# Seven half products in place of eight for 18 weight pairs of the first layer's feed-forward input, and a folded sequence transform

## The reference

```python
def ffn_sublayer(x, shift, scale, gate, g_pre, g_post, w_ffn_in, w_ffn_out):
    h = modulate(rmsnorm(x, g_pre), shift, scale)
    a, u = jnp.split(h @ w_ffn_in, 2, axis=-1)
    y = (jax.nn.silu(a) * u) @ w_ffn_out
    return x + gate * rmsnorm(y, g_post)

def fourier_mix(u):            # real part of the 2-D DFT over positions and channels, per channel group
    uf = u.astype(jnp.float32).reshape(b, l, FOURIER_GROUPS, w // FOURIER_GROUPS)
    return jnp.fft.fft2(uf, axes=(1, 3), norm="ortho").real
```

## Time and profile before

| | |
|---|---|
| three timed runs | median 1761.64 us (1760.34 to 1761.86) |
| profiled execution | 1760.17 us |
| its span | 1758.4 us |
| granted TensorE clock, mean | 0.976 |
| TensorE busy with matmuls | 1653.8 us (94%) |
| VectorE, ScalarE, GpSimd busy | 666.6 us, 516.1 us, 572.2 us |

### The profile page before, as it was taken

How to read it: one execution, slowest core, us unless ns; L and a number is a source line. 1 busy time by engine, 2 the same in 40 slices (tenths; PEclk the granted TensorE clock), 3 DMA queues, 4 the chain that set the end, 5 groups by cost and what they waited for, 6 DMA issues and landing times.

```text
span 1758.4 us, 22457 instructions
## 1 busy us (share of the span) xinstructions
PE 1653.8 (94%) x9084; PEld 1330.8 (76%) x9084; DVE 666.6 (38%) x847; ACT 516.1 (29%) x752; POOL 572.2 (33%) x259
## 2 busy tenths in 40 slices
PE   5899999999899999999999988999988899999995
PEld 1677877876688888888888746888765688888884
DVE  2510226768721211211111795126747422122136
ACT  3524113523522111221122245342422422222220
POOL 1412222134423222232222443233213444444432
PEclk9899999999899999999999999999999999999998
DMA  9334332135321121111211373122153233333331
GB/s 373 140 125 155 120 135 93 37 132 195 121 81 60 61 71 61 60 60 63 69 60 60 108 260 137 49 84 73 61 204 108 61 97 94 95 97 94 95 105 62
DMA packets 46331, 185.18 MB, mean 105 GB/s; under 512 B 4854, under 2 KB 7798, under 8 KB 39608
## 3 DMA queue, kind: packets, MB, share of 16 engines
q1 hardware_dynamic: 42444, 172.63, 29.7%
q10 hardware_dynamic: 3820, 11.60, 1.7%
HBM read 175.83 MB, written 8.39 MB: 105 GB/s over the span
## 4 chain that ended last, share of the span: by engine, by line
PE 61%; issue 19%; DVE 8%; POOL 5%; ACT 2%; DMA 2%; SPq 1%; POOLq 0%; DVEq 0%; ACTq 0%
PE A L636 55%; POOL w_lo L591 5%; DVE x L1327 2%; DVE y L1334 1%; DVE y L1326 1%; PE A L808 1%; PE A L802 1%; DMA raw<-modw 1%; DVE h_lo L1339 1%; PE N L873 1%; DVE sqb L1301 1%; PE G L777 1%; PE A L816 1%; ACT h_hi L1076 1%; SPq L555 1%
## 5 line engine op out<-in xcount | busy, mean ns | idle before, releaser
L591 POOL TENSOR_TENSOR w_lo<-raw,w_hi 128x1024 fp32r<-128x1024 f32 (+1 forms) x219 | 524.6, 2397 | 1074.4 <-ACT w_hi L897 1074.3
L636 PE MATMUL A<-h_hi,w_hi 128*128 128x512 f32 (+1 forms) x1808 | 571.0, 363 | 30.0 <-DVE h_lo L1339 21.3
L636 PE MATMUL A<-h_lo,w_hi 128*128 128x512 f32 (+1 forms) x1808 | 559.4, 357 | 0.0
L636 PE MATMUL A<-h_hi,w_lo 128*128 128x512 f32 (+1 forms) x1808 | 558.4, 356 | 0.0
L897 ACT ACTIVATE w_hi<-raw 128x1024 fp32r<-128x1024 f32 (+1 forms) x219 | 228.1, 1042 | 818.4 <-PE A L636 781.9
L636 PEld LDWEIGHTS A<-h_hi,w_hi 128*128 128x128 f32 x1808 | 306.7, 190 | 107.5 <-issue 27.9
L636 PEld LDWEIGHTS A<-h_lo,w_hi 128*128 128x128 f32 x1808 | 309.1, 191 | 49.3 <-issue 0.2
L636 PEld LDWEIGHTS A<-h_hi,w_lo 128*128 128x128 f32 x1808 | 307.3, 191 | 51.4
L1311 DVE TENSOR_TENSOR sqb<-sqb,A 128x768 f32<-128x768 f32 (+1 forms) x44 | 36.1, 821 | 427.2 <-PE A L636 426.9
L636 PE MATMUL A<-g_hi,w_hi 128*128 128x512 f32 (+1 forms) x528 | 168.5, 359 | 1.0 <-DVE y L1298 0.4
L636 PE MATMUL A<-g_hi,w_lo 128*128 128x512 f32 (+1 forms) x528 | 167.4, 356 | 0.0
(11 more groups left out here) (131 smaller groups left out, 1157.4 us busy)
## 6 DMA issues: line engine op xcount, KB each, us to landing
raw<-stream SPq DMA_DIRECT2D x219, 512.0 KB, 3.5
mraw<-modw SPq DMA_DIRECT2D x42, 1024.0 KB, 5.1
raw<-modw SPq DMA_DIRECT2D x6, 1024.0 KB, 14.8
x<-x_keep ACTq DMA_DIRECT2D x4, 1536.0 KB, 8.9
x_keep<-x SPq DMA_DIRECT2D x4, 768.0 KB, 21.4
x<-xT SPq DMA_DIRECT2D x1, 2048.0 KB, 8.5
x_keep<-x ACTq DMA_DIRECT2D x2, 1024.0 KB, 9.3
out_dram<-x ACTq DMA_DIRECT2D x4, 512.0 KB, 2.8
```

The costliest lines, as they stand in the source:

```text
L591: pool.tensor_tensor(w_lo[:, n % RING, 0:WIDTH[n]], raw[:, n % RAW, 0:WIDTH[n]], w_hi[:, n % RING, 0:WIDTH[n]].bitcast(F32), ALU.subtract) ...
L636: m = pe.matmul(dst[:, t0:t1], a, b[:, k, t0:t1], start=(first and p == 0), stop=(last and p == 2))
```

## The change

**Feed-forward input of the first layer.** The first four pairs stay as they are. For each of the other 18 the K axis (1024) and the 768 tokens are halved, and the two weight tiles `a` and `u` form the third halving: a 2 x 2 times 2 x 2 product. It is done by Strassen's method in Winograd's form: seven products of a weight quarter (512 x 128) with an activation quarter (512 x 384), each in three passes over four K tiles, 84 matmuls of 384 columns. Four weight sums (`w_sum`) are made for each pair and four activation sums T1 to T4 once. The seven results go round through eight PSUM banks and are joined by additions. Both weight tiles of a pair lie in the two `raw` buffers, from a new array `pairs`.

```diff
+FAST = 4
+LOW_P, LOW_S = (0, 1, 2, 5, 6), (3, 4)
+READ_ACT, READ_DVE = (0, 3), (1, 2, 4, 5, 6)
@@ SyncE, in its loop over the chunks
+                    if n == n_out(b):
+                        sp.wait_ge(lo_done, n)
+                        for pair in fast_pairs(b):
+                            q = pair - FAST
+                            if q:
+                                sp.wait_ge(f_lo, 5 * q)
+                                sp.wait_ge(sums_ready, 4 * q)
+                            for j in range(2):
+                                sp.dma_start(raw[:, j, :], pairs[q, :, j, :]).then_inc(pair_in, 16)
@@ GpSimd
+                        for pos in LOW_P:
...
+                            pool.wait_ge(f_hi, 7 * q + pos + 1)
+                            if pos == 2:
+                                pool.wait_ge(sums_ready, 4 * q + 4)
+                            pool.tensor_tensor(lo, src, f_weight(w_hi, q, pos).bitcast(F32), ALU.subtract).then_inc(f_lo, 1)
@@ TensorE
+                    moving = [h_block(0, 0), h_block(1, 0), t_block(2), h_block(0, 1), t_block(3), h_block(1, 1), t_block(4)]
+                    def product(q, pos):
...
+                        for k in range(4):
+                            cols = slice(k * P, (k + 1) * P)
+                            for a, b, p in ((wh, hi, 0), (wh, lo, 1), (wl, hi, 2)):
+                                m = pe.matmul(dst, a[:, cols], b[:, k, :], start=(k == 0 and p == 0),
+                                              stop=(k == 3 and p == 2))
+                        m.then_inc(f_used, 1)
...
+                        if i == 0:
+                            for u in ("A0", "A1") if e[2] else ("A0", "A1", "N0", "N1", "G0", "G1"):
+                                pe.wait_ge(free[u], PLAN.acc[e][u])
@@ TensorE, ffn_out
+                    if L == 0:
+                        pe.wait_ge(f_got, 2 * (sum(BLOCKS[:e[2] + 1]) - FAST))
+                        pe.wait_ge(f_sum, 5 * (sum(BLOCKS[:e[2] + 1]) - FAST))
@@ ScalarE, one pair
+                act.wait_ge(f_used, at + 1)
+                act.activation(part, bank(q, 0), ACT.Copy).then_inc(f_got, 1)
+                if not last:
+                    fast_hi(q + 1, 0)          # waits for pair_in of pair q + 1
+                act.wait_ge(f_used, at + 2)
...
+                act.wait_ge(f_used, at + 4)
+                act.wait_ge(g_ready, q + FAST + 1)
+                act.activation(up[:, hi_half], bank(q, 3), ACT.Copy).then_inc(f_got, 1)
+                    for pos in (2, 3, 4):
+                        fast_hi(q + 1, pos)
+                act.wait_ge(f_sum, summed(q, 5))
+                act.activation(sil[:, 0:TOK], sil[:, 0:TOK], ACT.Silu).then_inc(f_silu, 1)
+                act.wait_ge(f_used, at + 6)
+                    fast_hi(q + 1, 5)
+                act.wait_ge(f_used, at + 7)
+                    fast_hi(q + 1, 6)
+                act.wait_ge(f_gated, q + 1)
+                act.activation(g_hi[:, gp:gp + 1, :], sqb[:, 0:1, :], ACT.Copy).then_inc(ghi_ready, 1)
@@ VectorE, one pair
+                dve.tensor_tensor(sil[:, lo_half], part, bank(q, 1), ALU.add).then_inc(f_sum, 1)
+                dve.tensor_tensor(part, part, bank(q, 2), ALU.add).then_inc(f_sum, 1)
+                    dve.wait_ge(f_used, at + 4)
+                    early_sums(q + 1)          # 2 of 512, wait for pair_in of pair q + 1
+                step(dve.tensor_tensor(sil[:, hi_half], part, up[:, hi_half], ALU.add), 1)
+                dve.tensor_tensor(part, part, bank(q, 4), ALU.add).then_inc(f_sum, 1)
+                    late_sum(q + 1, 4)
+                step(dve.tensor_tensor(up[:, hi_half], part, up[:, hi_half], ALU.add), 2)
+                dve.tensor_tensor(sil[:, hi_half], sil[:, hi_half], bank(q, 5), ALU.add).then_inc(f_sum, 1)
+                    late_sum(q + 1, 5)
+                    sum_low(q + 1, 3)
+                    sum_low(q + 1, 4)
+                dve.tensor_tensor(up[:, lo_half], part, bank(q, 6), ALU.add).then_inc(f_sum, 1)
+                dve.tensor_tensor(sil[:, 0:TOK], sil[:, 0:TOK], up, ALU.mult).then_inc(f_gated, 1)
+                dve.tensor_tensor(g_lo[:, gp:gp + 1, :], sqb[:, 0:1, :], g_hi[:, gp:gp + 1, :].bitcast(F32),
+                                  ALU.subtract).then_inc(g_ready, 1)
```

**Room for the sums.** T2 and T3 lie where `x` is, so `x` is written to DRAM before the feed-forward block and read back at its last `ffn_out`. VectorE waits for that write before its first activation sum, and that stands ahead of its part of the first pairs:

```diff
+                elif kind == "spill":                                     (ScalarE, behind tail(0, 0))
+                    for s in range(0, KT, 4):
+                        act.dma_start(x_keep[:, s:s + 4, :], x[:, s:s + 4, :]).then_inc(x_kept, 16)
+                elif kind == "ffn_in" and L == 0:                         (VectorE)
+                    dve.wait_ge(x_kept, 96)
...
+                    t_sums(1)          # 4 x 384 elements each
+                    t_sums(3)
+                    t_sums(2)
+                    for q in range(FAST):
...
```

**Folded sequence transform.** Cosine and sine sums of a real sequence are even and odd in the output position. The `dft` chunks now hold only 258 of 512 (130 of 256) columns, the two sums go into PSUM columns of their own, and VectorE joins them:

```diff
-                    w = CTX if ctx_part else SEQ
+                    w = HALF_CTX if ctx_part else HALF_SEQ
@@ ORDER, among the attention tiles
             order.append(("score", L, tt))
+            if a == 0:
+                order.append(("halves", L))
...
             order.append(("o", L, tt))
+            if a == 0:
+                order.append(("fold", L))
```

More of the change, by code:

```diff
@@ L46, with fast_pairs, normal_pairs @@
 PB, PG, PCW, PCB, PGN, PCOLS = 0, 48, 80, 86, 88, 92
+FAST = 4
+HALF = TOK // 2
+LOW_P, LOW_S = (0, 1, 2, 5, 6), (3, 4)
+READ_ACT, READ_DVE = (0, 3), (1, 2, 4, 5, 6)
+def fast_pairs(b):
+    first = sum(BLOCKS[:b])
+    return range(max(first, FAST), first + BLOCKS[b])
+def normal_pairs(L, b):
+    first = sum(BLOCKS[:b])
+    return range(first, min(first + BLOCKS[b], FAST) if L == 0 else first + BLOCKS[b])
 def tiles_of(L):
@@ L215, in build_order @@
         tail(L, 0)
+        if L == 0:
+            order.append(("spill", 0))
         first = 0
         for b, nb in enumerate(BLOCKS):
-            order.append(("ffn_in", L, b, first))
+            if normal_pairs(L, b):
+                order.append(("ffn_in", L, b, first))
+            if L == 0:
+                order.append(("fast", L, b))
             order.append(("ffn_out", L, b))
@@ L240, in chunks_of @@
         out = []
[L241 removed]
+        for p in normal_pairs(L, e[2]):
             out += [("fin", L, p), ("fin", L, HID + p)]
@@ L374, in piece_before, with bass_hybrid_block @@
 def piece_before(p):
+    if PIECES[p][1:3] == (1, 1) and PIECES[p][3] < 2:
+        return PLAN.n0[("ffn_out", 0, 2)] + RAW + RING
     return PLAN.n0[PIECES[p - 2]] + RAW + RING - 1
-def bass_hybrid_block(nc: bass.Bass, stream, modw, xT, pos_row, pos_col, cols, wdec, masks, mats, wide, x_keep, out):
+def bass_hybrid_block(nc: bass.Bass, stream, pairs, modw, xT, pos_row, pos_col, cols, wdec, masks, mats, wide, x_keep, out):
     with ExitStack() as ctx:
@@ new lines, in y_block, with h_block, t_block, n_out @@
+        def y_block(k2, t2):
+            return y[:, 4 * k2:4 * k2 + 4, HALF * t2:HALF * t2 + HALF]
+        def h_block(k2, t2):
+            return [t[:, 4 * k2:4 * k2 + 4, HALF * t2:HALF * t2 + HALF] for t in (h_hi, h_lo)]
+        def t_block(j):
+            return [t[j] for t in (T_hi, T_lo)]
+        def n_out(b):
+            return PLAN.n0[("ffn_out", 0, b)]
+        def ring_half(q, pos):
+            b = next(b for b in range(len(BLOCKS)) if q + FAST in fast_pairs(b))
+            h = (2 * (n_out(b) % RING) + pos) % (2 * RING)
+            return h // 2, slice(h % 2 * 512, h % 2 * 512 + 512)
@@ L913, in _, with fast_hi, first_hi @@
             act.wait_ge(eps_set, 1)
+            def fast_hi(q, pos):
+                src = {0: A_RAW[1, 1], 1: A_RAW[1, 2], 6: A_RAW[2, 2]}
+                if pos in src:
+                    act.wait_ge(pair_in, 32 * (q + 1))
+                else:
+                    act.wait_ge(sums_ready, 4 * q + {3: 2, 2: 2, 4: 3, 5: 4}[pos])
+                src = src.get(pos, ring_f(q, pos))
+                act.activation(f_weight(w_hi, q, pos), src, ACT.Copy).then_inc(f_hi, 1)
+            def first_hi(b, step):
+                act.wait_ge(chunk_used, n_out(b) - 3 + step)
+                for pos in ((0, 1), (2, 3), (4, 5), (6,))[step]:
+                    fast_hi(fast_pairs(b)[0] - FAST, pos)
@@ L978, in _ @@
                 elif kind == "dft":
-                    end = e[2] == (3 if L else 4)
-                    if not end:
+                    if chunk_kind(n0 + RING) == "dft":
                         high(n0 + RING)
@@ L1435 @@
         "stream": stream_layout(a),
+        "pairs": pair_layout(a),
         "modw": mod_layout(a),
```

365 lines of the change are left out of this document (325 added, 40 removed).

## The result

| | before | after |
|---|---|---|
| timed runs | 1761.75 us median of 4 (1760.34 to 1762.37) | 1777.88 us median of 4 (1771.77 to 1781.81) |
| ratio, 95% interval | | 1.0087 (1.0070 to 1.0104) |
| profiled execution, granted clock | 1760.17 us, 0.976 | 1771.77 us, 0.969 |
| TensorE busy | 1653.8 us | 1623.5 us |

TensorE has 30 us less to do, and the program is 11.6 us longer in the profiled execution, 16 in the median. The chain of waits, by engine, answers to the earlier trace rows: the share of "issue" fell from 19% to 5%, and VectorE (8% before), DMA (2%) and ScalarE (2%) have larger shares, as TensorE itself has (61%).

What follows compares the result with a forecast made beforehand. It took TensorE's own instruction stream to bound the kernel; 1760.2 - 40.7 + 9.6 + 6.2 + 8 + 2 - 7 = 1738.3, and with 1.5 for the median 1739.8 us, range 1720 to 1766.

Steps and rivals of the forecast that it cites:

- term 2: Feeding the 18 pairs: the loop through the `raw` buffers takes 16.3 us, six late pairs lose 9.6 us in all.
- Term 1: The 18 pairs on TensorE: 84 matmuls of 384 columns at 0.175 each, 14.7 us per pair, 40.7 us won.
- rival D: TensorE's clock falls in the fast pairs' gaps of 1.6 us, for a quarter of that time: 1756 us, chance 0.04.
- term 3: Seams at starts and ends of the three pair blocks: TensorE waits for PSUM buffers and last additions, 6.2 us lost.
- Term 4: Writing x to DRAM before the activation sums: TensorE stands 5.9 us before chunk 3, then a slower clock, 8 us lost.
- Term 5: Norm in two steps: four tiles get a second ScalarE instruction, about half hidden in idle time, 2 us lost.
- Term 6: Folded transform in both layers: 11.4 us leave TensorE, 2.2 charged per layer among the attention tiles, 7 us won.
- A: The loop through `raw` never binds, as collisions are rarer or DMAs land sooner: 1730 us, chance 0.24.
- B: VectorE and GpSimd collide at full length, the loop through `raw` takes 19.3 us: 1771 us, chance 0.16.
- C: The fold brings nothing and the gap at the first block is 13 us: 1752 us, chance 0.14.

Runs made afterwards that it cites:

- E1: Third weight-half buffer, in a free part of `mraw`, added to the changed kernel: 1739.36 us, ratio to before 0.9883.
- E11: Changed kernel with two low parts per pair left out on VectorE and filled by two ScalarE copies: 1778.88 us.
- E10: Changed kernel, still with one pair of raw buffers, given finer waits at the six seams: 1762.6 us, ratio to before 1.0006.
- E5: Kernel before with the norm in two steps, x written to DRAM, waited for and read back, no activation sums: 1768.76 us.
- E7: E1's kernel with the activation sums and their wait for x moved behind VectorE's work for pair 0: 1738.28 us.
- E4: Kernel before with only the first layer's second norm done in two steps through `y`: 1768.4 us, ratio 1.0034.
- E8: E7's kernel with the norm in one step again and `y` completed afterwards: 1728.09 us.
- E3: Kernel before with the folded sequence transform alone: 1757.44 us, ratio 0.9979.

## Why the prediction was wrong, step by step

I forecast 1740 us and faster at 0.79. It came out at 1777.88, outside my range of 1720 to 1766, and slower. The step that failed is term 2, and within it the account of when the loop binds.

**Term 1, 18 pairs at 0.175: right.** With the third buffer a pair takes 14.72 us, so its 84 matmuls start 0.175 apart. The 18 pairs bring 39.7 us (305.3 at 16.96, 265.6 in E1's three blocks).

**Term 2, +9.6: measured 31.** The three blocks of pairs, from the first product to the end of the last, take 64.5, 133.3 and 98.8 us, the seam waits of 3.0, 3.0 and 1.3 taken off. In E1's kernel, where no pair waits, the same stretches take 59.1, 118.0 and 88.5, so the loop costs 31 us. Both factors were off. The period is 17.6 where I had 16.3: the fourth sum comes 7.0 after the landing (I said 6.1), the three low parts take 5.3 (4.95), the DMA 5.2 (5.1 + 0.1). Of the first part the collisions are what I had too small: L1452 and L1515 take 2.15 us more than their 0.69 and 0.55, where I had charged 1.0. (The 3.6 us of the chain is right for four instructions of 384; the text counts three.) And the stock in hand was 2.9 us, not 4.6. VectorE makes the early sums of the next pair behind its wait for product 3, so in a block's first pair they begin 2.8 us after the landing. In the second block, whose first product starts at 680.4, the landing is at 686.22 and the sums come here (timelines of VectorE and GpSimd):

```profile
689.06 0.96 DVE L1450 TENSOR_TENSOR w_sum<-raw 128x512 f32<-128x512 f32 x1 [1.53 <-PE G L1035]
...
694.64 3.32 POOL L783 TENSOR_TENSOR w_lo<-w_sum,w_hi 128x512 fp32r<-128x512 f32 x2 [5.17 <-DVE w_sum L1461]
```

The third weight is ready at about 696.4, 16.0 after the first product; I had 14.3. A stock of 2.9 and an excess of 2.9 per pair cover one pair, not three. So the loop binds from the fourth pair of a block (in the first block the third already waits 1.0): ten waits in place of six. The loop, 17.6, lay inside my bounds of 14.0 to 19.3; I had it as "the middle" and let the stock hide what a longer one does.

**Clock falls, 0.04 for rival D: there, but not shown to cost anything.** Windows of 5 to 6 us behind the last pairs' waits of the three blocks:

```profile
597.00:602.00 5.00, 4.89 (x19) 4.92 (x20) 3.85 (x5) 1.22 (x2) 3.62 (x2) 0.66 0.08 12
...
800.00:806.00 6.00, 4.64 (x18) 4.67 (x19) 4.85 (x6) 2.02 (x4) 4.86 (x3) 0.72 0.07 8
971.00:977.00 6.00, 5.90 (x25) 5.93 (x26) 4.52 (x6) 1.23 (x2) 3.61 (x2) 0.72 0.21 59
```

At these clocks the matmuls take about 1.7 us longer in each window. But the end of a block does not hang on them. In E11's profile the granted clock stays at 1.00 behind these three waits, and the blocks' pairs take 289.2 us in place of 296.5; TensorE then waits 13.4 us in place of 7.3 for VectorE's last additions. In the second block the last addition comes at 815.51 there and at 815.68 in the changed kernel. It hangs on the landing of the stream's first chunk (term 3). So what the falls take from term 2 they seem to give back in term 3, and the sum of the two, 31 + 12, is the firmer number. The rule that I weighed for D (the Trainium skill, "TensorE: Matmul & The Clock Gate", A second HAM failure mode) is so far borne out: with gaps of 2.3 us between groups of matmuls the clock falls now and then. In E1's kernel, which goes round the same eight banks without them, it stayed at 1.00 for all three blocks. So the gaps matter and the cycling alone does not. It is not a quarter of the time, as I had priced it.

**Term 3, seams +6.2: measured 12.4**, and 9.0 to 15.3 come back when the waits go (E10). The starts were right (1.2 each). The ends were not: 8.9 us where I had 2.6. The timeline of the first block's last pair:

```profile
604.32 1.06 ACT L1105 ACTIVATE w_hi<-raw 128x1024 fp32r<-128x1024 f32 x1 [3.59 <-issue]
605.29 0.47 ACT L1161 ACTIVATE sqb<-A 128x384 f32<-128x384 f32 x1
605.46 5.05 POOL L743 TENSOR_TENSOR w_lo<-raw,w_hi 128x1024 fp32r<-128x1024 f32 x2 [4.84 <-ACT w_hi L1105]
...
605.79 2.50 DVE L1515 TENSOR_TENSOR sqb<-mrow,sqb 128x384 f32<-128x384 f32 x1 [3.00 <-ACT sqb L1161]
...
608.91 2.02 DVE L1521 TENSOR_TENSOR sqb<-mrow,sqb 128x384 f32<-128x384 f32 x1
```

ScalarE's copy of product 3 (L1161) stands behind `w_hi` of the stream's first chunk, whose DMA is issued only after the pair's last low part. Two additions behind that copy then meet GpSimd's low parts of the stream, 2.50 and 2.02 us, and TensorE stands for 3.05 us until the last addition is done.

**Term 4, spill +8: measured a gap of 2.7**, and 0.4 for write and wait alone (E5). x landed 11.5 after the issue (I said 12), but I held the chunk before it for punctual: TensorE was ready for chunk 3 at 497.6 and not at 492.8, about 5 us late behind the norm in two steps, and that hid half of the stall. With the slower matmuls behind it the stall costs 3.7 us by the stage's length (E7).

**Term 5, norm in two steps +2: measured 6.5** (E4); 10.2 came back in E8, with E7's scatter in it. I took half as hidden in ScalarE's idle time. But TensorE waits tile by tile there, and the clock falls behind it.

**Term 6, fold -7: measured -4.5** (E3), the right sign. Matmuls of 130 columns cost 0.112 each, where I had scaled to 0.068, so 24 of them cost 1.1 us more than I had (rows of the changed kernel below; the earlier trace rows for the stage). The rest is in the attention tiles. In E3's profile the transforms are 5.4 and 5.2 us shorter, but from their start to `wout` only 1.9 and 2.9 are left, so the tiles lose 3.6 and 2.3 where I had charged 2.2 each:

```profile
301.58 0.28 PE L941 MATMUL A<-w_hi,h_lo 128*128 128x130 f32 x1
301.69 0.28 PE L941 MATMUL A<-w_hi,h_hi 128*128 128x130 f32 x1
```

**The sum again**, for the profiled execution: 1760.2 - 39.7 + 31 + 12 (12.4 less the 0.4 of before) + 2.7 + 6.5 - 4.5 = 1768.2 against 1771.8. The missing 3.6 us aren't assigned; 1.7 of them lie between `wout` and the first fast pair. The end of the tail and the head, which answer to the earlier trace rows, stood at a clock of 0.75:

```profile
462.00:489.00 27.00, 21.48 (x92) 17.18 (x91) 16.42 (x33) 14.35 (x30) 8.02 (x6) 0.75 0.30 114
```

The median's further 6.1 us go with a clock of 0.965 to 0.966 in the other runs.

**Rivals.** A fell: the loop binds. B is the nearest, with its time (1771) and its sign right. Its mechanism was half right, and its time is near by luck: at 17.6 the loop eats 31 of the 39.7 us that the pairs bring, and seams and norm take the rest; full-length collisions (19.3) were not needed. C was not it: the fold brought 4.5 and the gap was small.

## What to carry to other kernels

A loop of one buffer pair (land, use, free, land) is a clock of its own. Its period against the engine's decides, and before counting on stock at its start, look at what the first instruction of the loop really waits for in its engine's order. When TensorE becomes faster than its feeders, first give the feed a third buffer and make each wait as narrow as the buffer it protects: those two edits turned +16 us into -35. An extra instruction on the path of a tile-by-tile handoff costs its length and then the clock behind it.
